# A mixture-of-experts kernel in which the first expert item has three strips of 32 rows instead of four

## What is computed

```python
def moe_swiglu(h, w_router, w_g, w_u, w_d):
    t = h.reshape(-1, D_MODEL)
    logits = (t @ w_router).astype(jnp.float32)
    top_v, top_i = lax.top_k(logits, TOP_K)        
    top_w = jax.nn.softmax(top_v, axis=-1)
    gate = jnp.sum(jax.nn.one_hot(top_i, N_EXPERTS, dtype=jnp.float32) * top_w[..., None], axis=1).astype(h.dtype)
    out = jnp.zeros_like(t)
    for e in range(N_EXPERTS):
        out = out + gate[:, e:e + 1] * swiglu(t, w_g[e], w_u[e], w_d[e])
    return out.reshape(shp)
```

## Time and profile before

| | |
|---|---|
| time, median of 3 runs | 1766.97 us (1766.16 to 1767.21) |
| span of the profiled execution (the profile has no other time for it) | 1766.0 us |
| TensorE busy (matmul) | 1675.5 us, 95% |
| VectorE, ScalarE, GpSimd busy | 638.3, 497.3, 91.8 us |
| read from HBM | 521.80 MB, 296 GB/s over the span |
| TensorE's granted clock, mean | 0.975 |
| chain that ended last | TensorE 80%, DMA 7%, VectorE 5% |

### The profile page before, as it was taken

The page is one execution under the profiler, slowest core; times in us unless marked ns, Lnnn a source line. Parts: engine busy times, 40 slices in busy tenths (PEclk is TensorE's granted clock), DMA queues, the critical chain, the costliest instruction groups (busy, mean ns, idle before and its releaser), DMA issues.

```text
span 1766.0 us, 30412 instructions
## 1 busy us (share of the span) xinstructions
PE 1675.5 (95%) x13565; PEld 1039.7 (59%) x13565; DVE 638.3 (36%) x1020; ACT 497.3 (28%) x793; POOL 91.8 (5%) x105
## 2 busy tenths in 40 slices
PE   5999998999999899998999988999999998899997
PEld 3899987999999789998533323333333332333333
DVE  3477675444444666766600020101101002011111
ACT  3445533434343535553200011111111111111111
POOL 4020041000000010022000000000000000000000
PEclk9999998999999999999899999999999999899999
DMA  9464587677766533445777899999998999999995
GB/s 351 135 244 150 192 299 238 219 272 254 278 234 229 186 134 135 163 162 179 311 276 298 321 385 409 416 410 411 408 402 354 368 397 414 408 414 413 403 412 221
DMA packets 159460, 525.51 MB, mean 298 GB/s; under 512 B 5205, under 2 KB 11571, under 8 KB 152161
## 3 DMA queue, kind: packets, MB, share of 16 engines
q1 hardware_dynamic: 157088, 519.68, 76.8%
q0 software_dynamic: 2240, 3.88, 0.9%
HBM read 521.80 MB, written 1.74 MB: 296 GB/s over the span
## 4 chain that ended last, share of the span: by engine, by line
PE 80%; DMA 7%; DVE 5%; SPq 3%; ACT 2%; POOL 1%; issue 1%; ACTq 0%; DVEq 0%; POOLq 0%
PE ps L1673 11%; PE ps L1675 11%; PE ps L1674 11%; PE ps L2211 10%; PE ps L2141 9%; PE ps L2136 6%; PE ps L2115 5%; DMA e_raw<-in_w_e_gate_dram 3%; SPq L551 3%; PE ps L1679 2%; PE ps L2152 2%; PE ps L2128 2%; DMA raw<-in_w_e_gate_dram 2%; PE ps L1737 2%; PE ps L2068 2%; DVE wlo L1057 1%
## 5 line engine op out<-in xcount | busy, mean ns | idle before, releaser
L1673 PE MATMUL ps<-acts_hi,whi 128*128 128x256 f32 x1600 | 464.9, 291 | 20.7 <-DVE acts_lo L1106 6.7
L1674 PE MATMUL ps<-acts_lo,whi 128*128 128x256 f32 x1600 | 455.9, 285 | 0.0
L1675 PE MATMUL ps<-acts_hi,wlo 128*128 128x256 f32 x1600 | 455.8, 285 | 0.0
L1673 PEld LDWEIGHTS ps<-acts_hi,whi 128*128 128x128 f32 x1600 | 310.0, 194 | 40.7 <-issue 27.3
L1057 DVE TENSOR_TENSOR wlo<-raw,whi 128x1024 fp32r<-128x1024 f32 (+1 forms) x220 | 264.9, 1245 | 178.3 <-ACT whi L675 178.0
L1674 PEld LDWEIGHTS ps<-acts_lo,whi 128*128 128x128 f32 x1600 | 310.2, 194 | 0.8 <-issue 0.7
L1675 PEld LDWEIGHTS ps<-acts_hi,wlo 128*128 128x128 f32 x1600 | 310.0, 194 | 0.0
L675 ACT ACTIVATE whi<-raw 128x1024 fp32r<-128x1024 f32 (+1 forms) x220 | 219.7, 1049 | 63.1 <-PE ps L1675 26.5
L2141 PE MATMUL ps<-e_raw,KTt 128*32 128x512 f32 x1128 | 164.9, 593 | 0.0
L2136 PE MATMUL ps<-e_raw,KTt 128*32 128x512 f32 x360 | 157.0, 592 | 1.3 <-DVE KTt L1643 0.6
L1643 DVE TENSOR_TENSOR big<-ps,big 96x512 f32<-96x512 f32 (+1 forms) x16 | 17.5, 1096 | 298.2 <-PE ps L2141 205.6
(11 more groups left out here) (328 smaller groups left out, 2066.8 us busy)
## 6 DMA issues: line engine op xcount, KB each, us to landing
e_raw<-in_w_e_gate_dram SPq DMA_DIRECT2D x40, 2048.0 KB, 16.8
e_raw<-in_w_e_up_dram SPq DMA_DIRECT2D x38, 2048.0 KB, 15.7
e_raw<-in_w_e_down_dram SPq DMA_DIRECT2D x36, 2048.0 KB, 19.2
raw<-in_w_ada_dram SPq DMA_DIRECT2D x24, 2048.0 KB, 8.1
raw<-in_w_in_dram SPq DMA_DIRECT2D x22, 2048.0 KB, 8.9
raw<-in_w_e_down_dram SPq DMA_DIRECT2D x20, 2048.0 KB, 16.3
raw<-in_w_e_up_dram SPq DMA_DIRECT2D x18, 2048.0 KB, 20.6
raw<-in_w_e_gate_dram SPq DMA_DIRECT2D x16, 2048.0 KB, 19.1
```

Of the source, the lines that this page charges most:

```text
L1673: mm(out, a_hi, b_hi, start=start, stop=False, skip_group_check=shared)
L1674: mm(out, a_hi, b_lo, start=False, stop=False, skip_group_check=shared)
L1675: return mm(out, a_lo, b_hi, start=False, stop=stop, skip_group_check=shared)
```

## The change

Item 0 gets three strips, so expert 0's capacity becomes 96 like that of ranks 1 to 4; the table's formula loses the threshold that gave expert 0 a fourth strip. The number of written-out items with three strips, `THREES`, goes from 4 to 5, which the loop's bounds take in.

```diff
-ITEM_STRIPS = (4, 1, 3, 3, 3, 1, 3, 2)
+ITEM_STRIPS = (3, 1, 3, 3, 3, 1, 3, 2)
...
-            ts(cap, order, 0.5, -float(STRIP), ALU.is_gt, ALU.mult)
-            link(ts(over, order, 4.5, -float(STRIP), ALU.is_gt, ALU.mult))
-            link(tt(cap, cap, over, ALU.add))
+            ts(cap, order, 4.5, -float(STRIP), ALU.is_gt, ALU.mult)
             link(ts(over, order, 5.5, -float(STRIP), ALU.is_gt, ALU.mult))
             link(tt(cap, cap, over, ALU.add))
-            link(ts(cap, cap, 4.0 * STRIP, None, ALU.add))
+            link(ts(cap, cap, 3.0 * STRIP, None, ALU.add))
```

## The result

The changed kernel takes 1838.26 us (median, 1836.56 to 1839.37) against 1766.57 us: a ratio of 1.0407 with a 95% interval of 1.0394 to 1.042, so it is slower by 72 us. The forecast was 1836.5, and the time is inside the range of 1830 to 1846. The profiled execution took 1838.5 us with a span of 1836.7, 70.7 more than the span before.

What follows compares the result with a forecast made beforehand. The expert part was taken as a weight stream at about 412 GB/s, decoupled from TensorE by nine buffers. 1766.0 + 107.5 - 37.0 - 2.1 + 1.1 = 1835.5; with the median 0.97 above span, forecast 1836.5 us, range 1830 to 1846.

Steps and rivals of the forecast that it cites:

- The ninth item: Expert 0's 15 overflow tokens make the loop run twice, rereading 44.04 MB of weights at the stream's pace: +107.5 us.
- The reading by the rate: Price of the extra loop item taken as 44.04 MB at the windows' 412 GB/s: 106.9 us.
- The reading of 108.0 us per 21 pieces: Price of the extra loop item from 42 pieces in 215.97 us between gate loads of items 5 and 7.
- Item 0: First expert item at three strips instead of four, compared with item 3: 37.0 us shorter.
- Ahead of item 0: Gather and ScalarE's copy before the first expert item shorten with 96 rows instead of 128: -2.1 us.
- at no cost: VectorE's earlier first multiply, ScalarE's extra moves and item 1's loads add nothing; about 5 us of VectorE's cover left.
- Item 1: Second expert item takes longer because the stream is less far ahead after three strips than after four: +1.1 us.
- the first rival: Routing gives expert 0 at most 96 tokens, so no extra loop item runs: 1729 us, 2.1% faster; chance 0.03.
- The loop's second turn: Rival: the taken backward branch opens gaps in the weight stream, 369 GB/s, 119.4 us, total 1848 us; chance 0.05.
- the stream was not ahead: Refers to the rival that item 8's pieces come as early as TensorE wants, costing 94.6 us, total 1824; chance 0.02.

Runs made afterwards that it cites:

- the kernel without a ninth item: The changed kernel with the table's old formula, so expert 0's 15 tokens past row 96 lose that expert's part: 1732.46 us, ratio 0.9814 to the kernel before.
- the three extra matmuls: Three unread matmuls of 256 columns ahead of the token count, added to the kernel before: 1765.79 us; with fifth and sixth items exchanged too, 1764.26 us.
- the kernel with the other order: The kernel before, four strips and eight items, with its fifth and sixth items exchanged: 1764.23 us, ratio 0.9995.

## Why the prediction was right, and where a step was not

**The ninth item** (107.5 forecast, 106.55 in the profile, 106.58 to 106.64 in three others). Right in its mechanism and nearly in its size. The reading by the rate, 106.9, was the better one, as the windows stayed at 412 GB/s. The reading of 108.0 us per 21 pieces was too high, and not for the reason that the prediction gave, a queue that runs dry at its end. The last two gate loads of item 7 did come 17.1 us apart before, and 15.7 with a ninth item behind them (1680.65 to 1696.34). But in the kernel without a ninth item, whose queue runs dry at the same place, it is 15.7 too. The first row is the kernel before, whose last gate load at 1731.90 stands in the earlier trace rows; the other two are the kernel without a ninth item:

```profile
1714.80 0.97 PE L2152 MATMUL ps<-e_raw,KTt 128*32 128x512 f32 x2 [2.02 <-DMA e_raw<-in_w_e_gate_dram]
...
1680.21 1.06 PE L2152 MATMUL ps<-e_raw,KTt 128*32 128x512 f32 x2 [2.82 <-DMA e_raw<-in_w_e_gate_dram]
...
1695.90 0.62 PE L2152 MATMUL ps<-e_raw,KTt 128*32 128x512 f32 x2 [2.90 <-DMA e_raw<-in_w_e_gate_dram]
```

And the same 42 pieces took 215.4 us in the changed kernel (1480.93 to 1696.34): this stretch runs some 1 us per item behind the ninth item's pace, with a ninth item behind it or without. Why, no run here tells. By the 358 GB/s per core of the Trainium skill ("DMA: Bandwidth & Descriptors", section "Where 436 GB/s comes from") the item would have cost 123 us, an estimate. It was rightly set aside: no run here shows that rate where the stream is the limit, and the price measured five times is 106.6.

**Item 0** (-37.0 forecast, -37.2). Right, and for its reason. The third step waits 2.05 us for the second hidden chunk where item 3 had 0.30 behind a scatter: taking the second scatter away gained nothing, as forecast. VectorE's first multiply comes at 879.79 after 7.36 us without work, so the cover under "at no cost" held, and with more to spare than the 5 us forecast.

**Ahead of item 0** (-2.1 forecast, +1.1). This step failed. It took the gather's 5.66 us against 3.74 for a matter of 128 against 96 rows. It is the clock. Both gathers are of 32 matmul records; the one ahead of item 0 starts with TensorE at its lower level:

```profile
855.00:859.00 4.00, 3.90 (x18) 3.93 (x19) 3.55 (x23) 0.00 (x0) 0.00 (x0) 0.50 0.95 395
...
855.10 6.22 PE L2066 MATMUL ps<-big 128*128 128x96 f32 x32 [0.18 <-DVE big L1516]
```

That is the changed kernel: 96 columns, 6.22 us. The clock comes back while the gather runs, and when it does sets the length. The first window is the kernel before, the second the changed one, and each is the one in which the clock rose:

```profile
857.00:859.00 2.00, 2.00 (x15) 2.00 (x14) 1.76 (x10) 0.00 (x0) 0.00 (x0) 0.70 1.01 406
...
859.00:861.00 2.00, 2.00 (x15) 2.00 (x14) 1.93 (x3) 0.00 (x0) 0.00 (x0) 0.70 1.02 406
```

The other executions give 6.57, 6.63 and 6.66 us for 96 columns, and for 128 columns 5.55, 5.64 and 6.68. Where the clock stood at its full level the gather took 3.81 us at 128 columns and, read from the same timeline view, 3.81 at 96 (3.74 in the chain of the earlier trace rows). At either level the width changes nothing, so the narrower gather is worth nothing. The +1.1 us are 0.73 from before the gather began (855.10 against 854.37), which the change does not touch, 0.58 from the clock, and 0.20 less for ScalarE's copy, as forecast.

**Item 1** (+1.1 forecast, +0.45). The direction was right and the size too high; the other kernels with three strips in item 0 have 80.7 to 81.0 us here, those with four 80.2 to 80.4, so the effect is 0.3 to 0.8 us.

**The rivals.** Without a ninth item the kernel is indeed faster, by 33 us: the first rival's mechanism is real and only its condition, 96 tokens or fewer for expert 0, is not met. The change turns on 15 tokens. The loop's second turn does not hold the stream back, and the stream was not ahead.

The forecast missed 1838.26 by 1.8 us. Of these, 1.2 are in the span: 3.2 too little ahead of item 0, 2.0 too much in all the other pieces. The other 0.6 is the difference between median and profiled span, 1.56 us after and 0.97 before. That the two large terms came out to within 1 us is the mechanism's doing; that the sum is so near is in part luck, since errors of both signs met and the start of item 0 alone lies between 857.88 and 862.65 us in the profiled executions without extra matmuls.

## What to carry to other kernels

A capacity that is lowered below what the data need does not cost the overflow's work, it costs a whole pass over the weights: count the rows of the real inputs before reckoning the gain, since a profile in which everything fits does not show by how much. In a pipeline where a stream and an engine take turns as the limit, price an extra item by the one that is the limit at its place, here 44 MB at 412 GB/s, and a shorter one by the engine's count at its own; both can be read from one trace. When two like operations differ in length, look at the granted clock in their windows before putting it down to their shapes.

## What the hardware showed that was not expected

TensorE's clock stood at its lower level (0.50, 1.2 GHz) when the gather ahead of item 0 began, in all profiled executions but one. In the kernel before it fell between 844 and 845, in which TensorE ran short matmuls of 8 columns and transposes and was busy all of the time; with the three extra matmuls it was back ahead of the gather in one execution and not in the other. And it fell within an item, with no pause of TensorE at all: at the end of item 3 of the kernel with the other order it was at 0.50 for some 5 us and below 1.00 for longer, with matmuls all the way, and that item took 124.02 us in place of 120.76.

```profile
1329.00:1333.00 4.00, 4.00 (x36) 4.00 (x33) 0.00 (x0) 0.00 (x0) 0.00 (x0) 0.88 1.07 443
1333.00:1338.00 5.00, 5.00 (x28) 1.31 (x31) 0.00 (x0) 0.38 (x1) 0.00 (x0) 0.50 0.97 401
```

It fell within the gather of the next item, which took 4.33 us here, and at the same gather in the other kernel with this order (4.19 us). The gathers of the later items in the kernel before took 3.76 to 3.81 us by the same view. Why it fell here these runs don't tell.
